# First loads of a decoder-layer kernel in another order: identity first, token tiles without a chain, tables and vectors later

## What is computed

```
h = RMSNorm(x);  z = h @ W_in  ->  q, k, v (512 each), x_rnn, y_rnn, g_attn, g_rnn (1024 each)
A: attention, 8 heads of 64, QK-norm, relative bias, top-3 past blocks of 256 and the own causal block
B: conv1d(4) -> gated linear recurrence on x_rnn, times GeLU(y_rnn)
x = x + W_out( sigmoid(g_attn) * (A @ P_attn) + sigmoid(g_rnn) * (B @ P_rnn) )
x = x + W_2( relu(RMSNorm(x) @ W_1)^2 )
```

## Time and profile before

| | |
|---|---|
| median of 3 runs | 2386.32 us |
| lowest run | 2385.94 us |
| profiled execution | 2392.58 us |
| span of its slowest core (core 6) | 2390.7 us |
| spans of the eight cores | 2374.7 to 2390.7 us |
| mean granted TensorE clock of the cores | 0.978 to 0.981 |

### The profile page before, as it was taken

One profiled execution on the slowest core, in us unless ns is written; L12 is line 12 of the kernel. 1 busy time (PEld: TensorE's weight loads), 2 busy tenths in 40 slices (PEclk: granted clock), 3 DMA queues, 4 the chain that ended last, 5 costly groups with the idle time before them and its releaser, 6 DMA issues.

```text
span 2390.7 us, 43783 instructions; the slowest of 8 cores (2374.7 to 2390.7 us)
## 1 busy us (share of the span) xinstructions
PE 2267.0 (95%) x14494; PEld 1105.3 (46%) x14494; DVE 1171.3 (49%) x2225; ACT 1333.0 (56%) x2345; POOL 612.7 (26%) x593
## 2 busy tenths in 40 slices
PE   2899989999999977999999999999999999999999
PEld 1444434344444433454555555554555455554444
DVE  1677678687787854545434333324233432332332
ACT  1666676667677645364646546564765475563111
POOL 1687644344443410201002101101100200111200
PEclk9899999999999986999999999999999999999999
DMA  6866924575763347346655655557455644644543
GB/s 140 222 208 197 185 64 110 103 141 124 142 124 89 130 141 218 105 137 198 175 153 184 172 176 178 158 152 229 130 168 172 188 146 151 190 151 141 169 166 123
DMA packets 194598, 373.44 MB, mean 156 GB/s; under 512 B 15507, under 2 KB 106684, under 8 KB 176316
## 3 DMA queue, kind: packets, MB, share of 16 engines
q1 hardware_dynamic: 188684, 336.04, 45.0%
q0 software_dynamic: 5696, 34.61, 10.1%
HBM read 332.30 MB, written 91.76 MB: 177 GB/s over the span
## 4 chain that ended last, share of the span: by engine, by line
PE 84%; DMA 5%; issue 4%; DVE 3%; POOL 2%; ACT 1%; SPq 0%; DVEq 0%; POOLq 0%; ACTq 0%
PE bank L475 84%; POOL s_ssq L475 1%; DMA s_pvec<-pvec 1%; DMA s_t1r<-t_s 1%; DMA s_xs<-x 1%; DMA rm_s<-s_t_0 1%; DMA s_qT<-s_mskT 1%; DMA outT<-s_x1T 1%; DVE s_cv L475 0%; SPq L480 0%; DVE s_ii L475 0%; DMA s_x1T<-xT 0%; ACT s_PT L475 0%; DVE s_ssq L475 0%; DVE s_t1r L475 0%
## 5 line engine op out<-in xcount | busy, mean ns | idle before, releaser
L475 ACT ACTIVATE s_PT<-bank 128x512 bf16<-128x512 f32 (+3 forms) x1152 | 590.9, 562 | 314.3 <-PE bank L475 195.1
L475 PE MATMUL bank<-s_uT,s_wsl 128*128 128x512 bf16 x2048 | 518.9, 379 | 1.5 <-DVE s_mskT L475 0.9
L475 PE MATMUL bank<-s_h2T,s_wsl 128*128 128x512 bf16 x2048 | 516.8, 380 | 0.8 <-DVE s_h2T L475 0.8
L475 PEld LDWEIGHTS bank<-s_Vr,s_PT 128*128 128x128 bf16 x4224 | 273.3, 98 | 267.1 <-issue 31.1
L475 PE MATMUL bank<-s_qT,s_kTr 80*128 80x512 bf16 (+3 forms) x1152 | 376.0, 370 | 9.2 <-ACT s_PT L475 4.0
L475 PE MATMUL bank<-s_Vr,s_PT 128*128 128x65 bf16 x4224 | 315.5, 195 | 12.1 <-ACT s_PT L475 11.7
L475 ACT ACTIVATE s_rl<-bank 128x512 f32<-128x512 f32 x256 | 152.9, 598 | 302.5 <-PE bank L475 293.8
L475 PEld LDWEIGHTS bank<-s_h2T,s_wsl 128*128 128x128 bf16 x2048 | 190.8, 98 | 180.8 <-issue 3.2
L475 PEld LDWEIGHTS bank<-s_uT,s_wsl 128*128 128x128 bf16 x2048 | 184.8, 98 | 164.3 <-issue 5.3
L475 DVE TENSOR_TENSOR s_uT<-s_rl 128x512 bf16<-128x512 f32 x176 | 122.9, 699 | 267.1 <-ACT s_rl L475 266.6
L475 DVE TENSOR_TENSOR s_x1T<-bank,s_x1T 128x512 f32<-128x512 f32 x128 | 88.2, 691 | 311.3 <-PE bank L475 310.7
(11 more groups left out here) (119 smaller groups left out, 2744.4 us busy)
## 6 DMA issues: line engine op xcount, KB each, us to landing
s_wsl<-wff_s SPq DMA_DIRECT2D x128, 1024.0 KB, 5.9
s_xs<-x SPq DMA_DIRECT2D x32, 512.0 KB, 5.3
wff_s<-wff_p POOLq DMA_DIRECT2D x16, 1024.0 KB, 15.2
s_rmr<-rm_s SPq DMA_DIRECT2D x64, 256.0 KB, 4.5
s_t1r<-t_s SPq DMA_DIRECT2D x64, 256.0 KB, 4.1
s_x1T<-xT SPq DMA_DIRECT2D x64, 256.0 KB, 4.7
outT<-s_x1T SPq DMA_DIRECT2D x64, 256.0 KB, 5.9
h_s<-s_hT SPq DMA_DIRECT2D x32, 256.0 KB, 4.1
```

The costliest lines, as they stand in the source:

```text
L475: return P.add(eng, lambda e, m=meth, kw=kw: getattr(e, m)(**kw), reads, writes, cost=c_, lat=lat, fam=fam, tag=tag or (writes[0] if write ...
```

## The change

Four things. The identity is loaded ahead of the first token tile. Token tiles 1 to 3 no longer wait for the load before them. `pvec`, `nwc` and `mtab` wait until the transposed tile 6 has been copied into its buffer, and the two inputs of the bias table until tile 8 has. And `schedule` has two pipes for transfers, one for each issuing queue, that take half the rate each while both have work.

```diff
-        pipe = 0.0
+        pipe = {"sync": 0.0, "gpsimd": 0.0}
...
             if o.dsem is not None:
-                pipe = max(pipe, s + cost) + o.nbytes / 280.0
-                fin = pipe + 2000.0
+                oth = "gpsimd" if e == "sync" else "sync"
+                st_ = max(pipe[e], s + cost)
+                part = min(o.nbytes, max(0.0, pipe[oth] - st_) * 140.0)
+                pipe[e] = st_ + part / 140.0 + (o.nbytes - part) / 280.0
+                pipe[oth] += part / 280.0
+                fin = pipe[e] + 2000.0
...
+        dma("sync", identb, cid_d, "c0a", [], ["identb"])
         load_x(0)
         dma("sync", nw, nw_d, "c0b", [], ["nw"])
-        dma("sync", identb, cid_d, "c0a", [], ["identb"])
         for j in range(3):
             dma("gpsimd", wqkv[j], wqkv_d[j].rearrange("p (a b) -> p a b", a=8), "wqkv%d" % j, [], ["wqkv%d" % j])
         for t in range(1, NXS):
-            load_x(t, P.after("nw") if t == 1 else P.after("xs%d" % (t - 1)))
+            load_x(t)
...
-        def bias_table():
+        def bias_table(late):
             op("vector", "memset", [], ["ii0"], ap=tabx[32:33, :], constant=NEG)
-            dma("sync", tabx[0:32, :], relb_d, "c1a", [], ["ii0"])
-            dma("sync", Gs[0:33, :], cG_d, "c1b", [], ["cv0"])
+            dma("sync", tabx[0:32, :], relb_d, "c1a", [], ["ii0"], extra=late)
+            dma("sync", Gs[0:33, :], cG_d, "c1b", [], ["cv0"], extra=late)
...
             if t == 6:
-                dma("sync", pvec, pvec_d.rearrange("p (t j) -> p t j", t=8, j=11), "c0c", [], ["pvec"])
-                dma("sync", nwc, nwc_d, "c0f", [], ["nwc"])
-                dma("sync", mtab, cm_d.rearrange("p (a b c) -> p a b c", a=3, b=16, c=16), "c0d", [], ["mtab"])
+                late = P.after("hT%d" % (t % NHT))
+                dma("sync", pvec, pvec_d.rearrange("p (t j) -> p t j", t=8, j=11), "c0c", [], ["pvec"], extra=late)
+                dma("sync", nwc, nwc_d, "c0f", [], ["nwc"], extra=late)
+                dma("sync", mtab, cm_d.rearrange("p (a b c) -> p a b c", a=3, b=16, c=16), "c0d", [], ["mtab"], extra=late)
...
             if t == 8:
-                bias_table()
+                bias_table(P.after("hT%d" % (t % NHT)))
```

## The result

The changed kernel takes 2371.38 us (median of 4 runs) beside 2386.71 us of the kernel before, a ratio of 0.9934 (95% interval 0.9915 to 0.9954): 15.3 us faster, less than two per cent. One of the four runs on each side (2642.07 and 2692.71 us) was in a slower state of the chip, and the ratio is of the fast runs alone. Forecast were 2367 us and 18.8 us. In a later comparison, beside two experiments, the ratio was 0.9938 (0.9924 to 0.9952).

What follows compares the result with a forecast made beforehand. PE was taken as the bound, with its early waits for the identity and a copy into `hT` recoverable. The front's mark moves from 71.53 to 52.7 us, saving 18.8: 2386.3 - 18.8 = 2367.5 us, range 2352 to 2386.

Steps and rivals of the forecast that it cites:

- the dense stretch: Front end: PE's projections start at 37.9 us and stay dense, all weights and four tiles being there.
- How loads and casts share the engines: Start: beside casts, an SP load of 128 rows takes one cast, about 6 to 8 us, whatever its size.
- rival 1: Front end: token tiles pass two to a cast, or `qkw` is not in the way; saving 26, 2360 us; chance 0.2.
- Identity first: Start: tile 0 and `nw` delayed by one 0.43 us issue; PE's 16.4 us wait goes, transposes at 10.8.
- Late loads: Front end: ACT copies tile 0 from 12 to 13 us instead of 29.29; no delay taken for tiles behind.
- Token tiles unchained: Front end: tiles 1, 2, 3 land at 17.6, 25.8, 33.2 us, `qkcol` at about 33.5 instead of 22.85.
- The planner's two pipes: Front end: `qkw` stands early in VectorE's queue, so VectorE and PE wait for `qkcol` from about 22 to 33.5 us.
- The sum: Front end: from 37.9 us, 14.8 us of PE work remain, reaching the 71.53 us mark at 52.7; 18.8 us saved.
- that point: Front end: 71.53 us in the kernel before, with 58 `wqkv` matmuls and five transpose sets done; forecast at 52.7 us.
- One slip: Front end: bound on removable idle time, at most some 35 us, so the 47.7 us of two per cent is unreachable.
- Rival 2: Front end after 71.53 us: tile loads reach PE's chain, two 5 us waits; saving 9, 2377 us; chance 0.13.
- Rival 3: Where attention begins, 800 to 1000 us: another order costs 23 us or more, 2391 us; chance 0.08.

Runs made afterwards that it cites:

- e1: Kernel before with only the five loads of `pvec`, `nwc`, `mtab` and the bias inputs made late; ratio 0.9942 (0.9927 to 0.9956), 13.9 us faster.
- x1: Changed kernel plus an unread 1 KB load of 128 rows between `nw` and tile 1; no total time given, tile 1 14.7 us after `nw`.
- x3: Changed kernel with VectorE's multiply of `qkcol` put behind the copy of tile 3; no total time given, PE busy 69.13 of first 100 us.
- e2: Kernel before with the late loads and the planner's two pipes, old order of identity and tiles, old chain; ratio 1.0001 (0.9992 to 1.001).

## Why the prediction was right

The forecast of 2367 us and the range held, and its main mechanism is shown: late `pvec` lets ACT copy tile 0, which e1 measures alone at 13.9 us. That the dense stretch begins at about 38 us, as forecast, is partly luck. `nw` and tiles 1 and 2 came some 7 us later than forecast, the wait for `qkcol` that was to hold PE holds nothing, and another wait, of ACT for tile 2, ended at nearly the same time.

*How loads and casts share the engines.* Right, and shown by itself: rows decide, not bytes. Token tiles did not pass two to a cast: tiles 1 and 2 are in 7.5 and 15.8 us after `nw`, so the first half of rival 1 falls. That half rested on the Trainium skill, DMA: Bandwidth & Descriptors, section "SWDGE vs HWDGE vs iDMA", which gives a packet as preferably at most 4096 bytes. These runs agree with the same page's turns packet by packet (section "Queues, rings and completion order") only if a whole row of a cast, longer than 4096 bytes, is one packet. The trace counts it so; the cast queue in the first 36 us of after (packets, MB, share of 16 engines):

```profile
q0 software_dynamic: 432, 3.15, 53.6%
```

Three casts of 128 rows are 384 rows of 8 KB, which make the 3.15 MB; the other 48 packets are 16 for each cast.

*Identity first.* This step failed. It said that tile 0 and `nw` are delayed by the issue of 0.43 us and the transposes start at 10.8. By the law of the step above it and the rows of before, the third load was to have the first cast's round, and I gave `nw`, now third, the place that it had had as second. It landed at 16.9, with the first cast; transposes at 18.55, first projection at 20.91 instead of 17.9. In e1, with the identity behind `nw`, the first projection is 2.3 us earlier.

*Late loads.* Right: copy of tile 0 straight behind the transposes, and nothing given back among the tiles behind. `pvec` was issued at 69.96, and in 60 to 100 us PE was busy 39.30 of 40. e1 measures the part alone: 13.9 us.

*Token tiles unchained.* The round was counted as one too few: tiles 1 and 2 at 24.4 and 32.7 instead of 17.6 and 25.8. Tile 3 (33.7; ACT takes it up at 34.66) and `qkcol` (33.9) came as forecast (33.2 and 33.5), since the last cast has landed by then (32.4). That tile 1 itself is early is worth nothing that can be seen at the last `wqkv` matmul (x1, one profile).

*The planner's two pipes.* VectorE's order was right, its effect not. The wait for `qkcol` is 5.3 us instead of 11, and x3 takes it away for nothing; so the second half of rival 1, that `qkw` is not in the way, came true, without its gain. What holds PE is ACT, whose order I had not followed: squares of tile 2 ahead of the copy of tile 1. It ends at the same time only because tile 2 (32.6) and `qkcol` (33.9) land close together.

*The sum.* By 38 us 15 matmuls were done where 16 were forecast by 33.5; 58 at 51.4 us against 52.7. The slow pace of 0.446 us a matmul ended with the second group, so the 3.5 us for two more slow groups fall away; of the 13.4 us from 38.0 on, 43 matmuls at 0.226 take 9.7, and transposes and waits 3.7 where 1.8 were counted. The saving at that point is 20.1 against 18.8 us, and, in the mean of the cores, 20.8 and 18.3 us (two profiles) at the last `wqkv` matmul. From there 2.3 and 2.9 us are lost at the step to the next stage (between: 70.4 and 71.0 against 68.1). The medians, which are of the slowest core, give 15.3 and, in the later comparison, 13.8. One slip changes nothing: 71.5 less 16 less 15 to 20 us leaves 35 to 40 us of idle time, not at most 35, and still less than two per cent.

*The rivals.* Rival 2 had a little of its mechanism come true, some 2 to 3 us, but in another place than forecast: not token loads between 50 and 100 us but GpSimd's cast behind a store, at 260 to 285 us. Its own mechanism shows in e2, where a token tile holds ACT between 75 and 100 us. Rival 3's place is unchanged (166.22 against 166.84 us), and the planner alone is 0.9996; the new plan does cost in e2, at the step to the next stage. Why e2 also falls behind between 75 and 100 us is only partly read (the wait of ACT for that tile); it was not tried by itself.

Whether after gains anything beyond the late loads alone (0.9934 against 0.9942, in separate comparisons) these intervals can't say.

## What to carry to other kernels

While casts are under way, count the loads that stand ahead of the one you need on its queue, by rows and not by bytes: moving a load to the front moves the loss to the one that is now in its place. When an early gain does not reach the end, look at the next stage for an engine that waits for a store in the order of its queue: a cast waited there for a late store to free its space, the multiply that PE needed stood behind it, and a 7 us gain was lost in full until that cast was moved. And an order planned for one arrangement of loads can cost under another: test parts together as well as alone.

## What the runs showed of the hardware

The first two SP loads go through before a cast does (the identity in 1.7 us, tile 0 in 5.0 us), the third takes 14.9 us, 512 KB or, in before, 32 KB (14.3). From then on one SP load of 128 rows lands with each cast, within some 0.2 us of it (16.9 and 16.7, 24.3 and 24.2, 32.6 and 32.4). A load of 1 KB beside three casts costs the next load 6.3 to 6.8 us as 128 rows and 1.0 to 1.4 us as 16 rows, in the mean of the cores, and nothing to a load that lands after the last cast.

A matmul of 128x512 takes 0.446 us at first (3.57 for 8 at 20.91) although the stretch has a granted clock of 1.00, that is 2.4 GHz; from the dense stretch on it is 0.226. Before the slow groups PE had done little but wait. The pace of the first groups is read from their durations, not from the granted clock of the row.
